# A fused stack of four layers on one core: the turns for the layer after the final norm move ahead of that norm, and one mixer's last splits and gates change place

## The chip, the cores and the metric

The kernel runs on 1 core of a Trainium2 chip. The time is the device time of one execution in microseconds (us), the median over runs. TensorE is PE in the profile (its weight loads are PEld), VectorE is DVE, ScalarE is ACT, GpSimd is POOL, and SyncE (SP) issues the weight transfers.

## The reference

`x` is 256 tokens by 1024 channels in float32. It goes through two stacks, one after the other. In short:

```python
def first_block(x, ...):
    for i in range(2):
        x = x + 0.5 * swiglu(rmsnorm(x, n1), wu1, wd1)
        h = rmsnorm(x, mix_norm[i])
        if i % 2 == 0:
            mix = mixer_delta_retention(h, ...)       # gated delta rule beside retention
        else:
            mix = mixer_dilated_differential(h, ...)
        x = x + mix
        x = x + 0.5 * swiglu(rmsnorm(x, n2), wu2, wd2)
    return rmsnorm(x, final_norm)

def second_block(x, ...):
    # layer 0
    hn = _rms_norm(h, e_norm_mix[i]);  ...  # gated unit beside an rwkv time mix
    h = h + _swiglu(_rms_norm(h, e_norm_ffn[i]), ...)
    # layer 1: sparse attention beside a short convolution, then 8 experts, 2 per token
    return _rms_norm(h, final_norm)
```

`rmsnorm(x, w)` is `x * rsqrt(mean(x*x) + 1e-6) * w`. The output of the first stack is normed by `final_norm`, and the first thing that the second stack does is to norm that again by `e_norm_mix`. The output of the delta mixer is, per head, normed, multiplied by a gate, and then multiplied by `l0_w_out`; the retention half has its own norm and gate.

## The kernel before, in words

`NETWORK` lists twelve layers: ffn 0, delta 1, ffn 2, ffn 3, attention 4, ffn 5, final 6, rwkv 7, ffn 8, sparse 9, moe 10, final 11 (the numbers are `at` in the code). Weights stream from HBM in steps of 128 x 3072 floats through a ring of three slots (`ring`, transfers issued at L3535 and L3541). Each step has three parts of 1024 columns. A float32 product is made from three passes of fp32r operands (L315 to L317: high by high, and the two high by low), so each part of each step is *split*: ACT rounds it to `w_hi` (`split_hi`, L283), then DVE subtracts for `w_lo` (`split_lo`, L290, parts 0 and 1) and POOL does the third part (`split_lo_last`, L296). PE waits for part 0 ahead of the first of a step's eight k blocks, for part 1 ahead of k = 2 and for part 2 ahead of k = 5.

The activations are wanted channel by partition, so PE transposes `X` by the identity (`head_tensor`, L406, 16 transposes in four pairs), ACT rounds and scales by the norm's gain (`head_scalar`, L414, 8 instructions) and DVE makes the low half (`head_vector`, L423, 8). The row norm itself is left out of the operand: PE multiplies the unscaled activations, while ACT sums the squares of `X` (`stats_scalar`, L432, L435), DVE takes the reciprocal (`stats_vector`, L442) and makes two diagonal matrices (L445), and PE turns these into a row (`row_tensor`, L452). In a mixer that begins with "t" tiles, as delta and rwkv do, `row_tensor` stands in PE's order between step 0 and step 1 of the projection. In DVE's order the split of step 1 stands ahead of `stats_vector`; in ACT's order the third part of step 1 (`split_hi(..., (2,))`) waits for the reciprocal.

Layer "final" (6) has nothing on PE. ACT sums squares per half of the tokens (`norm_scalar`, L337 to L344), DVE takes the reciprocal and overwrites `X` with the normed and gained rows (L348, L908). Only then does PE transpose `X` for rwkv; ahead of that it issues 16 matmuls whose result nobody uses (`keep_warm`, L329).

Delta's end: `inverse_tensor` and its partners on DVE and ACT invert eight 128 x 128 triangles in six levels. Each level is a product Y (L999), a copy by ACT (L960), a product dU (L1011), a subtraction by DVE (L937), a transpose back (L990) and a copy by DVE (L945). `ahead={...}` puts other DVE work ahead of a level's subtraction and `at_level={...}` puts other work into the level's middle. In level 6 PE turns retention's gated outputs of both token tiles (`turns((0, 1), 4)`, L1086) between Y and dU. After the levels come the delta rule's own products, a gate per token tile (`normalise`) and the output projection, whose first step `g` and second step `g + 1` are split meanwhile. `out_part` and `rest` are its products; the last of them, `rest(1)`, waits for the turned and split tile "delta hT 1 0".

## Time and profile before

| | |
|---|---|
| median of 3 runs | 2033.1 us (2032.88 to 2034.56) |
| the profiled execution | 2032.94 us, its span 2031.0 us |
| PE busy | 98% of the span |
| DVE, ACT, POOL busy | 76%, 57%, 20% |
| mean busy share of the DMA engines | about 57% |
| PE's granted clock over the span | 0.993 of full |

A timeline row gives the start, the length, the engine, the line, the operation, what is written and read, the count of instructions that are merged in the row, and in brackets how long the engine stood idle before it and for whom. PE's clock has two levels, 1.2 and 2.4 GHz; a granted clock of 0.5 is the lower.

### The profile page before, as it was taken

The page shows a single profiled execution, that of the slowest core. Times are in us where ns is not written, and L with a number is a line of the kernel's source. Part 1 is how long each engine was busy: PE and PEld are TensorE (multiplying, and loading weights), DVE is VectorE, ACT ScalarE, POOL GpSimd, SP SyncE. Part 2 cuts the span into 40 slices and gives each one's busy share as a digit, 9 for nine tenths or more (in the row PEclk, how much of TensorE's full clock was granted, in tenths as well). Part 3 has the DMA queues.
Part 4 walks back from the last instruction along what each step waited for, and adds up shares of the span by engine and source line. Part 5 has one row for each costly group of instructions (what it writes and reads, how often), then busy time and mean ns, then how long its engine had stood idle before and what let it go on. Part 6 is the DMA issues. An engine that isn't in the chain of part 4 may idle for free.

```text
span 2031.0 us, 31723 instructions
## 1 busy us (share of the span) xinstructions
PE 1981.4 (98%) x11697; PEld 1747.0 (86%) x11697; DVE 1551.4 (76%) x2173; ACT 1152.6 (57%) x1707; POOL 396.9 (20%) x192
## 2 busy tenths in 40 slices
PE   8999998999999999999999999999999999999997
PEld 6888998888888899988889898888998788888885
DVE  6777886777777778677778767777786798888886
ACT  5445664544554455654456535444566677777775
POOL 2222032322222310233222341322002000000000
PEclk9999999999999999999999999999999999999998
DMA  9555531555565544455544004555553688888895
GB/s 354 188 190 191 171 110 63 187 193 193 173 192 195 192 167 156 146 187 186 187 168 164 1 1 167 197 191 192 186 207 116 238 315 324 320 328 325 327 333 183
DMA packets 73395, 401.21 MB, mean 198 GB/s; under 512 B 8256, under 2 KB 8384, under 8 KB 41152
## 3 DMA queue, kind: packets, MB, share of 16 engines
q1 hardware_dynamic: 72848, 398.07, 56.3%
q8 instruction: 76, 1.25, 0.2%
q10 hardware_dynamic: 432, 1.57, 0.2%
q14 instruction: 39, 0.32, 0.0%
HBM read 398.57 MB, written 1.05 MB: 197 GB/s over the span
## 4 chain that ended last, share of the span: by engine, by line
PE 86%; DVE 8%; PEld 3%; ACT 2%; issue 1%; DMA 0%; SPq 0%; ACTq 0%; DVEq 0%; PEldq 0%
PE psum L777 20%; PE psum L315 15%; PE psum L316 14%; PE psum L317 14%; PE psum L757 10%; PE psum L1011 2%; DVE w_lo L290 2%; PE psum L999 2%; PE psum L3102 1%; PEld psum L315 1%; PEld psum L317 1%; PEld psum L316 1%; PE psum L329 1%; DVE w_lo L296 1%; PE psum L2358 1%
## 5 line engine op out<-in xcount | busy, mean ns | idle before, releaser
L290 DVE TENSOR_TENSOR w_lo<-ring,w_hi 128x1024 fp32r<-128x1024 f32 x498 | 739.7, 1515 | 175.2 <-ACT w_hi L283 173.9
L283 ACT ACTIVATE w_hi<-ring 128x1024 fp32r<-128x1024 f32 x744 | 739.9, 1051 | 206.1 <-PEq L509 106.2
L296 POOL TENSOR_TENSOR w_lo<-ring,w_hi 128x1024 fp32r<-128x1024 f32 x132 | 326.0, 2470 | 1098.0 <-ACT w_hi L283 1098.0
L777 PE MATMUL psum<-fT,w_hi 128*128 128x512 f32 x1760 | 421.9, 391 | 3.8 <-ACT w_hi L283 3.8
L777 PEld LDWEIGHTS psum<-fT,w_hi 128*128 128x128 f32 x1760 | 330.3, 189 | 72.0 <-ACT w_hi L283 4.2
L315 PE MATMUL psum<-w_hi,hT_hi 128*128 128x384 f32 (+4 forms) x896 | 321.1, 358 | 4.4 <-DVE hT_lo L1325 2.0
L317 PE MATMUL psum<-w_hi,hT_lo 128*128 128x384 f32 (+4 forms) x896 | 310.3, 346 | 0.0
L316 PE MATMUL psum<-w_lo,hT_hi 128*128 128x384 f32 (+4 forms) x896 | 310.0, 346 | 0.0
L315 PE MATMUL psum<-w_hi,act_hi 128*128 128x512 f32 x596 | 234.5, 393 | 0.8 <-DVE act_lo L3382 0.7
L757 PEld LDWEIGHTS psum<-fT,w_lo 128*128 128x128 f32 x1760 | 226.0, 191 | 8.9
L316 PE MATMUL psum<-w_lo,act_hi 128*128 128x512 f32 x596 | 233.5, 392 | 0.0
L317 PE MATMUL psum<-w_hi,act_lo 128*128 128x512 f32 x596 | 232.4, 390 | 0.0
L757 PE MATMUL psum<-fT,w_lo 128*128 128x256 f32 x1760 | 228.7, 283 | 0.0
L842 ACT ACTIVATE up_sums<-psum 128x512 f32<-128x512 f32 x110 | 65.6, 596 | 234.4 <-PE psum L757 234.4
L315 PEld LDWEIGHTS psum<-w_hi,hT_hi 128*128 128x128 f32 x896 | 169.3, 189 | 22.0 <-DVE w_lo L290 5.7
L317 PEld LDWEIGHTS psum<-w_hi,hT_lo 128*128 128x128 f32 x896 | 169.1, 189 | 13.5
L316 PEld LDWEIGHTS psum<-w_lo,hT_hi 128*128 128x128 f32 x896 | 169.6, 189 | 9.8 <-issue 0.2
L296 DVE TENSOR_TENSOR w_lo<-ring,w_hi 128x1024 fp32r<-128x1024 f32 x113 | 137.7, 1218 | 2.0 <-ACT w_hi L283 2.0
L844 ACT ACTIVATE silu<-silu 128x256 f32<-128x256 f32 x110 | 45.9, 417 | 162.8 <-DVE silu L876 162.8
L317 PEld LDWEIGHTS psum<-w_hi,act_lo 128*128 128x128 f32 x596 | 112.0, 188 | 24.5
L315 PEld LDWEIGHTS psum<-w_hi,act_hi 128*128 128x128 f32 x596 | 112.4, 189 | 23.4 <-issue 2.0
L316 PEld LDWEIGHTS psum<-w_lo,act_hi 128*128 128x128 f32 x596 | 112.4, 189 | 19.1
(507 smaller groups left out, 2384.2 us busy)
## 6 DMA issues: line engine op xcount, KB each, us to landing
ring<-in_stream SPq DMA_DIRECT2D x249, 1024.0 KB, 5.4
ring<-in_stream SPq DMA_DIRECT2D x248, 512.0 KB, 4.3
tables<-in_tables SPq DMA_DIRECT2D x1, 2261.0 KB, 19.8
gain_row<-in_gains ACTq DMA_DIRECT2D x3, 512.0 KB, 3.7
rows<-in_rows SPq DMA_DIRECT2D x1, 1288.0 KB, 22.7
X<-in_x SPq DMA_DIRECT2D x1, 1024.0 KB, 4.9
result<-X SPq DMA_DIRECT2D x2, 512.0 KB, 3.3
columns<-in_columns SPq DMA_DIRECT2D x1, 993.0 KB, 15.0
```

The source lines that it names most:

```text
L283: act.activation(part(w_hi, g, i), ring[:, k, i * PART:(i + 1) * PART], ACT.Copy) \
L290: dve.tensor_tensor(part(w_lo, g, i), ring[:, k, i * PART:(i + 1) * PART], part(w_hi, g, i).bitcast(F32), ALU.subtract) \
L296: pool.tensor_tensor(part(w_lo, g, 2), ring[:, k, 2 * PART:STEP], part(w_hi, g, 2).bitcast(F32), ALU.subtract) \
L315: pe.matmul(out_, w[0], x[0], start=first, stop=False, skip_group_check=True)
L316: pe.matmul(out_, w[0], x[1], start=False, stop=False, skip_group_check=True)
L317: return pe.matmul(out_, w[1], x[0], start=False, stop=last, skip_group_check=True)
L757: ins = pe.matmul(psum[:, 4 + 2 * (s % 2) + o, 0:SEQ], w[1][:, o, k, :], fT_hi[:, k, :], start=False, stop=k == KT - 1, skip_group_check=True)
L777: pe.matmul(psum[:, 4 + 2 * (s % 2) + o, :], w[0][:, o, k, :], fT[:, k, :, :].rearrange("p a c -> p (a c)"), start=k == 0, stop=False, ski ...
L842: act.activation(up_sums[:, s % 2, :, :], up_half(s, 1), ACT.Copy).then_inc(ffn_extra_kept, 1)
L844: act.activation(silu[:, s % 2, :], silu[:, s % 2, :], ACT.Silu).then_inc(ffn_silu_ready, 1)
L999: ins = pe.matmul(b[:, m * P:(m + 1) * P], AM[:, 4 * c + m, :], U[:, 4 * c + m, :], start=True, stop=True)
L1011: ins = pe.matmul(b[:, m * P:(m + 1) * P], T[:, 4 * c + m, :], Y[:, 4 * c + m, :], start=True, stop=True)
```

## The change

It has two parts. **Around the final norm**: PE's 16 transposes for rwkv (layer 7) read `X` as ffn 5 leaves it, ahead of the final norm, right after ffn 5's last product. The rounding then scales by `joint_gain`, the product of the two gains, computed once on DVE. The final norm of `X` is done behind these on ACT and DVE, as rwkv's row factor needs the squares of the normed `X`; that factor is then multiplied by the final norm's own (`rstd_f`), one DVE instruction more. The 16 `keep_warm` matmuls go. **In delta's end**: retention's gate of the second token tile (`retention_gated(1)`, 4 instructions) stands ahead of level 6 instead of level 5; part 0 of step `g` is split behind the levels instead of ahead of level 6; its third part is split by POOL, once level 5 is done, instead of by DVE; and for step `g + 1` the turned tile's rounding and its low half stand ahead of the last part that each of ACT and DVE splits.

```diff
@@ rstd_vector @@
-            dve.reciprocal(rstd[:, t:t + 1], rms[:, t:t + 1]).then_inc(*norm.vector())
+            dve.reciprocal(rstd_f[:, t:t + 1], rms[:, t:t + 1]).then_inc(*norm.vector())
@@ gain_of @@
+        def after_final(n):
+            return n > 0 and NETWORK[n - 1][0] == "final"
+
         def gain_of(n):
+            if after_final(n):
+                return joint_gain
             return columns[:, KT * NETWORK[n][1]:KT * (NETWORK[n][1] + 1)]
@@ head_tensor @@
-                        pe.wait_ge(*after(f"x {n} {t} {k}"))
+                        pe.wait_ge(*after(f"x {n - after_final(n)} {t} {k}"))
@@ stats_vector @@
             dve.reciprocal(rstd[:, :], rms[:, :]).then_inc(*norm.vector(f"norm {n} rstd"))
             dve.wait_ge(*norm.vector.so_far())
+            if after_final(n):
+                dve.tensor_tensor(rstd[:, :], rstd[:, :], rstd_f[:, :], ALU.mult).then_inc(*norm.vector(f"norm {n} rstd"))
+                dve.wait_ge(*norm.vector.so_far())
@@ ffn_tensor @@
-            if NETWORK[at + 1][0] != "final":
-                head_tensor(pe, at + 1)
+            head_tensor(pe, at + 1 + (NETWORK[at + 1][0] == "final"))
@@ final_vector @@
             for t in range(TT):
                 rstd_vector(dve, at, t)
-            for t, ins in enumerate(gained(dve, at, X)):
+            dve.wait_ge(*after(f"norm {at + 1} turn {PAIRS[-1]}"))
+            for t, ins in enumerate(gained(dve, at, X, rstd_f)):
@@ delta_scalar @@
-            split_hi(act, g + 1, g + 1)
+            split_hi(act, g + 1, g + 1, (0, 1))
             turned_hi(1, 0)
+            split_hi(act, g + 1, g + 1, (2,))
@@ delta_pool @@
             inverse_pool(pool, "delta", d_A, d_AM)
-            out_pool(pool, at, first=1)
+            pool.wait_ge(*after(f"delta U {LEVELS - 2} 1"))
+            out_pool(pool, at)
@@ delta_vector @@
-            def retention_gated():
-                dve.wait_ge(*after("delta ret root"))
-                does(None, dve.reciprocal, d_ret_rms, d_ret_rms)
-                dve.wait_ge(*after("delta rg"))
-                settle()
-                for t in range(TT):
+            def retention_gated(t):
+                if t == 0:
+                    dve.wait_ge(*after("delta ret root"))
+                    does("delta ret inverse", dve.reciprocal, d_ret_rms, d_ret_rms)
+                    dve.wait_ge(*after("delta rg"))
+                    settle()
+                for t in (t,):
...
-                           ahead={2: retention_scores, 3: weighted_gate, 4: retention_sums, 5: retention_gated, 6: lambda: split_lo(dve, g, g, (0,))})
+                           ahead={2: retention_scores, 3: weighted_gate, 4: retention_sums, 5: lambda: retention_gated(0), 6: lambda: retention_gated(1)})
             turned_lo(0, 4)
             turned_lo(1, 4)
-            split_lo(dve, g, g, (1,))
-            dve.wait_ge(hi_last_ready, g + 1)
-            dve.tensor_tensor(part(w_lo, g, 2), ring[:, in_ring(g, g)[0], 2 * PART:STEP], part(w_hi, g, 2).bitcast(F32), ALU.subtract) \
-               .then_inc(lo_last_ready, 1)
+            split_lo(dve, g, g)
...
-            split_lo(dve, g + 1, g + 1)
+            split_lo(dve, g + 1, g + 1, (0,))
             turned_lo(1, 0)
+            split_lo(dve, g + 1, g + 1, (1,))
@@ tensor block @@
-                elif NETWORK[at - 1][0] == "final":
-                    keep_warm(pe, psum[:, 7, :], 16)
-                    head_tensor(pe, at)
@@ scalar block @@
                         load_gain_row(act, n)
+                        head_scalar(act, at + 1)
                         norm_scalar(act, at)
@@ vector block @@
+                    dve.tensor_tensor(joint_gain[:, :], col("gain")[:, KT * 6:KT * 7], col("gain")[:, KT * 10:KT * 11], ALU.mult) \
+                       .then_inc(*norm.vector("joint gain"))
                 if kind == "final":
                     if NETWORK[at - 1][0] != "moe":
+                        head_vector(dve, at + 1)
                         final_vector(dve, at)
```

On DVE, from the end of ffn 5 to rwkv's first copies, before:

```order
L894 SCALAR_TENSOR_TENSOR X<-psum,rstd_f,X 128x512 x4
L348 RECIPROCAL rstd<-rms 128x1 x2
L908 SCALAR_TENSOR_TENSOR X<-X,rstd,gain_row 128x1024 x2
L423 SCALAR_TENSOR_TENSOR hT_lo<-psum,columns,hT_hi 128x256 x8
L2634 MEMSET r_pb 128x14
L2634 TENSOR_TENSOR columns<-columns,tables 128x512
L290 TENSOR_TENSOR w_lo<-ring,w_hi 128x1024 x2
L442 RECIPROCAL rstd<-rms 128x2
L445 TENSOR_SCALAR O<-tables,rstd 128x128 x2
```

and in the changed kernel, whose lines stand some numbers further down:

```order
L905 SCALAR_TENSOR_TENSOR X<-psum,rstd_f,X 128x512 x4
L432 SCALAR_TENSOR_TENSOR hT_lo<-psum,joint_gain,hT_hi 128x256 x8
L349 RECIPROCAL rstd_f<-rms 128x1 x2
L919 SCALAR_TENSOR_TENSOR X<-X,rstd_f,gain_row 128x1024 x2
L2647 MEMSET r_pb 128x14
L2647 TENSOR_TENSOR columns<-columns,tables 128x512
L291 TENSOR_TENSOR w_lo<-ring,w_hi 128x1024 x2
L451 RECIPROCAL rstd<-rms 128x2
L454 TENSOR_TENSOR rstd<-rstd,rstd_f 128x2
L457 TENSOR_SCALAR O<-tables,rstd 128x128 x2
```

The eight low halves of the turned `X` moved ahead of the final norm's three steps; the split of rwkv's step 1 still stands between the final norm and the diagonals.

On ACT at the same place, before:

```order
L283 ACTIVATE w_hi<-ring 128x1024 x3
L901 DMA gain_row<-in_gains 128x1024
L337 ACT_TABLE_LOAD
L337 ACTIVATE warm<-tables 128x1
L341 ACTIVATE O,squares<-X 128x1024
L344 ACTIVATE rms<-squares,tables 128x1
L341 ACTIVATE O,squares<-X 128x1024
L344 ACTIVATE rms<-squares,tables 128x1
L414 ACTIVATE hT_hi<-psum,columns 128x256 x8
L429 ACTIVATE warm<-tables 128x1
L432 ACTIVATE O,squares<-X 128x1024 x2
```

and in the changed kernel:

```order
L284 ACTIVATE w_hi<-ring 128x1024 x3
L912 DMA gain_row<-in_gains 128x1024
L423 ACTIVATE hT_hi<-psum,joint_gain 128x256 x8
L338 ACT_TABLE_LOAD
L338 ACTIVATE warm<-tables 128x1
L342 ACTIVATE O,squares<-X 128x1024
L345 ACTIVATE rms<-squares,tables 128x1
L342 ACTIVATE O,squares<-X 128x1024
L345 ACTIVATE rms<-squares,tables 128x1
L438 ACTIVATE warm<-tables 128x1
L441 ACTIVATE O,squares<-X 128x1024 x2
```

The eight roundings moved ahead of the table load and the final norm's squares.

On DVE in delta's last levels (levels 5 and 6 and what follows), before:

```order
L1325 RECIPROCAL d_small<-d_small 128x8
L1325 SCALAR_TENSOR_TENSOR O<-O,d_small,d_tok 128x128 x8
L937 TENSOR_TENSOR d_U<-d_U,psum 128x512 x2
L945 COPY d_T<-psum 128x512 x2
L290 TENSOR_TENSOR w_lo<-ring,w_hi 128x1024
L937 TENSOR_TENSOR d_U<-d_U,psum 128x512 x2
L1325 TENSOR_TENSOR hT_lo<-psum,hT_hi 128x4x128 x2
L290 TENSOR_TENSOR w_lo<-ring,w_hi 128x1024
L1473 TENSOR_TENSOR w_lo<-ring,w_hi 128x1024
L1325 COPY O<-psum 128x512
```

and in the changed kernel:

```order
L1339 RECIPROCAL d_small<-d_small 128x8
L1339 SCALAR_TENSOR_TENSOR O<-O,d_small,d_tok 128x128 x4
L949 TENSOR_TENSOR d_U<-d_U,psum 128x512 x2
L957 COPY d_T<-psum 128x512 x2
L1339 SCALAR_TENSOR_TENSOR O<-O,d_small,d_tok 128x128 x4
L949 TENSOR_TENSOR d_U<-d_U,psum 128x512 x2
L1339 TENSOR_TENSOR hT_lo<-psum,hT_hi 128x4x128 x2
L291 TENSOR_TENSOR w_lo<-ring,w_hi 128x1024 x2
L1339 COPY O<-psum 128x512
```

Four of the eight gate instructions took the place of the split ahead of the last subtraction; behind it two splits stand as before, and the third is gone to POOL.

## Rows read from the trace of the kernel before

**Rows 1.** The page: busy time of PE, and the chain that ended last, by engine.

```profile
PE 1981.4 (98%) x11697; PEld 1747.0 (86%) x11697; DVE 1551.4 (76%) x2173; ACT 1152.6 (57%) x1707; POOL 396.9 (20%) x192
PE 86%; DVE 8%; PEld 3%; ACT 2%; issue 1%; DMA 0%; SPq 0%; ACTq 0%; DVEq 0%; PEldq 0%
```

**Rows 2.** Timeline from ffn 5's last product to rwkv's first.

```profile
1038.24 0.61 PE L802 MATMUL psum<-w_hi,act_lo 128*128 128x512 f32 x2
...
1039.01 3.61 PE L329 MATMUL psum<-tables 128*128 128x512 bf16 x16
...
1041.27 1.04 ACT L341 ACTIVATE O<-X 128x1024 f32<-128x1024 f32 x1
...
1043.03 2.48 DVE L908 SCALAR_TENSOR_TENSOR X<-X,rstd,gain_row 128x1024 f32<-128x1024 f32 x2
...
1048.63 0.37 PE L315 MATMUL psum<-hT_hi,w_hi 128*128 128x256 f32 x1
```

**Rows 3.** Timeline of rwkv's first two steps, engine by engine.

```profile
1047.38 3.37 DVE L423 SCALAR_TENSOR_TENSOR hT_lo<-psum,columns,hT_hi 128x256 fp32r<-128x256 f32 x8 [1.86 <-ACT hT_hi L414]
...
1051.27 2.36 DVE L290 TENSOR_TENSOR w_lo<-ring,w_hi 128x1024 fp32r<-128x1024 f32 x2
...
1053.74 0.48 DVE L445 TENSOR_SCALAR O<-tables,rstd 128x128 f32<-128x128 f32 x2
...
1054.88 2.39 POOL L296 TENSOR_TENSOR w_lo<-ring,w_hi 128x1024 fp32r<-128x1024 f32 x1 [15.82 <-ACT w_hi L283]
...
1056.89 0.61 PE L452 MATMUL psum<-O,tables 128*128 128x128 f32 x4
...
1059.10 0.28 PE L315 MATMUL psum<-hT_hi,w_hi 128*128 128x256 f32 x1
```

**Rows 4.** Timeline of another passage, from ffn 0 straight to delta.

```profile
198.81 0.62 PE L802 MATMUL psum<-w_hi,act_lo 128*128 128x512 f32 x2
...
201.54 0.36 PE L315 MATMUL psum<-hT_hi,w_hi 128*128 128x256 f32 x1
...
199.97 3.03 ACT L414 ACTIVATE hT_hi<-psum,columns 128x256 fp32r<-128x256 f32 x8 [0.95 <-PE psum L406]
203.01 1.28 ACT L429 ACT_TABLE_LOAD   x1
```

**Rows 5.** Timeline of delta's levels 5 and 6, and of its end.

```profile
322.40 2.19 DVE L1325 SCALAR_TENSOR_TENSOR O<-O,d_small,d_tok 128x128 f32<-128x128 f32 x8
...
328.23 0.69 DVE L945 COPY d_T<-psum 128x512 f32<-128x512 f32 x1 [0.64 <-PE psum L990]
...
347.32 0.68 DVE L1325 TENSOR_TENSOR hT_lo<-psum,hT_hi 128x512 fp32r<-128x512 f32 x1
...
343.65 2.94 ACT L283 ACTIVATE w_hi<-ring 128x1024 fp32r<-128x1024 f32 x3
...
325.29 1.13 PE L999 MATMUL psum<-d_U,d_pad 128*128 128x128 f32 x8 [1.89 <-issue]
...
328.02 1.04 PE L1086 MATMUL psum<-tables,O 128*128 128x128 f32 x8
328.90 1.95 PE L1011 MATMUL psum<-d_Y,d_T 128*128 128x128 f32 x16
...
345.46 0.60 PE L1086 MATMUL psum<-tables,O 128*128 128x128 f32 x4
348.06 0.45 PE L315 MATMUL psum<-w_hi,hT_hi 128*128 128x384 f32 x1 [2.00 <-DVE hT_lo L1325]
```

**Rows 6.** Windows: span of time, its length, busy time by engine, PE's granted clock.

```profile
349.00:352.00 3.00, 3.00 (x11) 3.00 (x10) 0.33 (x1) 0.00 (x0) 0.64 (x1) 0.50 0.84 344
...
1045.10:1048.40 3.30, 2.83 (x14) 2.84 (x15) 1.44 (x4) 1.87 (x5) 0.00 (x0) 0.51 0.00 0
```

**Rows 7.** Timeline of one step of ffn 5, POOL and DVE side by side.

```profile
1028.37 2.41 POOL L296 TENSOR_TENSOR w_lo<-ring,w_hi 128x1024 fp32r<-128x1024 f32 x1 [5.87 <-ACT w_hi L283]
...
1029.27 3.72 DVE L290 TENSOR_TENSOR w_lo<-ring,w_hi 128x1024 fp32r<-128x1024 f32 x2 [1.37 <-ACT w_hi L283]
```

More of the change, by code:

```diff
@@ L68, in __getitem__ @@
         return slice(*self.at[name])
-COLUMN = Places([("gain", 10 * KT), ("conv", 4 * 12), ("mu", 14), ("w0", 4), ("a0", 4), ("k_k", 4), ("k_a", 4),
+COLUMN = Places([("gain", 11 * KT), ("conv", 4 * 12), ("mu", 14), ("w0", 4), ("a0", 4), ("k_k", 4), ("k_a", 4),
                  ("r_k", 4), ("sgu_b", 4), ("sgu_w", 4 * P), ("router", KT * EXPERTS), ("lora", 512), ("g2", 512),
@@ L137, in network_kernel @@
         rstd_f = sb("rstd_f", [P, TT])
+        joint_gain = sb("joint_gain", [P, KT])
         rstd_diag = O[:, 0, 0:TT * P].rearrange("p (t c) -> p t c", t=TT)
@@ L411, in head_scalar @@
                 act.wait_ge(*after(f"norm {n} turn {p}"))
+                if after_final(n):
+                    act.wait_ge(*after("joint gain"))
                 for i in range(2):
@@ L443, in stats_vector @@
             dve.wait_ge(*norm.vector.so_far())
+            if after_final(n):
+                dve.tensor_tensor(rstd[:, :], rstd[:, :], rstd_f[:, :], ALU.mult).then_inc(*norm.vector(f"norm {n} rstd"))
+                dve.wait_ge(*norm.vector.so_far())
             for t in range(TT):
@@ L901, in load_gain_row, with gained @@
             act.dma_start(gain_row[:, :], gains_in[which].partition_broadcast(P)).then_inc(row_loaded, 16)
-        def gained(dve, at, to):
+        def gained(dve, at, to, scale=rstd):
             dve.wait_ge(row_loaded, 16 * sum(kind in ("final", "moe") for kind, _ in NETWORK[:at + 1]))
             for t in range(TT):
-                yield dve.scalar_tensor_tensor(to[:, t, :], X[:, t, :], rstd[:, t:t + 1], gain_row[:, :], ALU.mult, ALU.mult)
+                yield dve.scalar_tensor_tensor(to[:, t, :], X[:, t, :], scale[:, t:t + 1], gain_row[:, :], ALU.mult, ALU.mult)
         def final_vector(dve, at):
@@ L3473, in _ @@
                         load_gain_row(act, n)
+                        head_scalar(act, at + 1)
                         norm_scalar(act, at)
                 elif kind != "moe":
-                    head_scalar(act, at, (3,) if after_mixer(at) else PAIRS)
+                    if not after_final(at):
+                        head_scalar(act, at, (3,) if after_mixer(at) else PAIRS)
                     if at == 0:
@@ L3498, in _ @@
                 if kind != "moe":
-                    head_vector(dve, at, (3,) if after_mixer(at) else PAIRS)
+                    if not after_final(at):
+                        head_vector(dve, at, (3,) if after_mixer(at) else PAIRS)
                     if at == 0:
@@ L3666, in pack_columns @@
     names = ["l0_ffn1_norm", "l0_mix_norm", "l0_ffn2_norm", "l1_ffn1_norm", "l1_mix_norm", "l1_ffn2_norm",
-             "e_norm_mix_2", "e_norm_ffn_2", "o_norm_mix_2", "o_norm_ffn_2"]
+             "e_norm_mix_2", "e_norm_ffn_2", "o_norm_mix_2", "o_norm_ffn_2", "final_norm"]
     c[:, COLUMN["gain"]] = np.concatenate([per(a[n].reshape(-1)) for n in names], axis=1)
```

## The prediction

> **What bounds the kernel now.** I read the page first, then the timeline where the change lies, then the windows for the clock. The page says that PE is busy for 98% of the span and that 86% of the chain that ended last is PE's [rows 1]. So a change can only give back time in which PE waits or runs at its lower clock; work taken from DVE or ACT counts for nothing by itself. There are two such places where the diff lies.
>
> The first is around the final norm. PE issues ffn 5's last product at 1038.24 and rwkv's first at 1048.63. Between them it runs 16 matmuls for nobody (3.61 us), then waits for ACT's squares and DVE's 2.48 us of rewriting `X`, since the transposes read the rewritten `X` [rows 2]. In the same trace ffn 0 passes straight to delta with the same 16 transposes: last product 198.81, first product 201.54, 2.73 us instead of 10.39 [rows 4].
>
> The second is delta's end. Y of level 6 starts at 325.29 after 1.89 us of idle, behind DVE's eight gate instructions (2.19 us), and the last product of the first output step starts at 348.06 after 2.00 us of idle [rows 5]. Behind that second gap the granted clock is 0.50, the level of 1.2 GHz; so it is behind the gaps of the final norm [rows 6].
>
> **The change, at the final norm.** The passage becomes that of ffn 0, moved by 1038.24 - 198.81 = 839.43. rwkv's first product then starts at 201.54 + 839.43 = 1040.97, 7.66 us earlier than now. The 16 idle matmuls cost nothing more. That is not the gain yet, because the row factor stands next in PE's order, 8.26 us after the first product (1048.63 to 1056.89 [rows 2, 3]): PE asks for it at about 1049.3, and it is now late. Its chain:
>
> - ACT ends the eight roundings and loads its table at 203.01 + 839.43 = 1042.44 for 1.28 us [rows 4]. That load was hidden under ffn 5's end before. The first square starts at about 1043.8. The second follows a square of 1.04 us, its reading and its root; I take 1.35, so 1045.15. From the second square's start to the rewriting of `X` took 1043.03 - 1041.27 = 1.76 [rows 2], so DVE starts at 1046.9 and ends 2.48 later, at 1049.4.
> - DVE then has the same work as now between the low halves and the diagonals: 1047.38 + 3.37 = 1050.75 to 1053.74, 2.99 us, of which 2.36 are the split of step 1 [rows 3]. ACT's second pair of squares ends beneath that split. The added multiplication of two columns I take at 0.25 us with its wait (bounds 0.1 and 0.5, the lengths of nothing but a small instruction and of both diagonals, 0.48). The diagonals start at 1052.65 and are done at 1053.1, against 1054.22 now.
> - So PE stands idle at the row from about 1049.3 to 1053.2, some 3.9 us, where before it did not wait.
> - Behind the row, step 1 wants its third part at k = 5, which it reaches 1059.10 - 1056.89 = 2.21 us after the row [rows 3]: 1055.4. But ACT rounds that part only after the reciprocal and the multiplication, and POOL's 2.39 us follow; POOL starts 1.14 after the diagonals start (1053.74 to 1054.88), so at 1053.8, and ends at 1056.2 [rows 3]. With a handover of 0.1, k = 5 starts at 1056.3, against 1059.10.
>
> That is 2.8 us, not 7.66. What the clock takes has to come off: behind gaps of two to three microseconds the lower clock lasted 3.3 us [rows 6], and this gap is longer. If it begins at the row, 3.3 us pass before full speed is back, half of it lost; PE has 0.9 us of slack to the third part, so 0.7 remains. I take 0.65, with bounds 0 (all of it falls in the gaps) and 1.65 (none does). The part gives 2.8 - 0.65 = 2.15. Queues passed: SP's transfers wait for the splits, which come earlier; the gain row's transfer stands before the moved roundings as before. The joint gain's instruction lies on DVE while it waits for ACT's first rounding behind ffn 0, and costs at most 0.1.
>
> **The change, in delta's end.** Four gate instructions are 1.10 us, so Y of level 6 starts at 324.2. But the other four stand now between DVE's last copy (328.92, now 327.8) and PE's turn of the second tile, which stands ahead of dU. The gate ends at 328.9, four transposes take half of 328.90 - 328.02, 0.44, and dU starts at 329.4: 0.5 us later than now, and not earlier [rows 5]. DVE then has two splits ahead of the copy of `o 0` as it had before, so everything behind comes 0.5 later. POOL's split of the third part begins at about 324.8 and is done by 327.8, long before PE asks; nothing waits for it.
>
> At the end ACT rounds the turned tile after two parts instead of three (0.98 us each). PE's transposes end at 345.46 + 0.60 = 346.06; from ACT being free to the low half took 347.32 - (343.65 + 2.94) = 0.73, and from there to PE's product 348.06 - 347.32 = 0.74 [rows 5]. So 347.5 instead of 348.06, plus the 0.5 from above: 348.0. The path gains 0.05 and the gap shrinks from 2.0 to 1.45 us. The two parts split later, ACT's third and POOL's behind it, are done at about 351.5 with the 0.5; PE asks for them near 352.6 at full clock.
>
> What remains is the clock. In three microseconds at 0.50 PE does half the work [rows 6]; 3.3 us minus the stretch's edges cost 1.5. The gap of 1.89 us ahead of level 6 was followed by full-length work at the higher clock (eight matmuls in 1.13, as elsewhere), the one of 2.00 was not [rows 5]. With 1.45 I expect the clock to stay up, and take 1.5 us; bounds 0 and 1.6.
>
> **Sum.** 2.15 + 0.05 + 1.5 = 3.7, less 0.1 for the joint gain: 3.6. Against the profiled execution's 2032.94 that is 2029.3; the median of the runs, 2033.1, is 0.16 above it, so I forecast 2029.4, 0.18% faster. A measurement of this kernel can tell about 0.2%, 4.1 us, from no change, so the likeliest case lies just inside "the same".
>
> A rule that speaks against the change: the Trainium skill, TensorE: Matmul & The Clock Gate, "Why this matters for your kernels", wants no long idle gap between bursts of matmuls, since the array falls back to its lower clock. The trace agrees: both low stretches follow gaps, one of them only 2.0 us long. By that rule the removed 16 matmuls and the new gap at the row are a risk, priced in the third rival.
>
> A second one: the Trainium skill, SBUF — State Buffer, "Who interferes with whom", says that POOL and a DVE instruction with both inputs in SBUF exclude each other for a whole instruction. The trace agrees: beside POOL's split, DVE's pair takes 3.72 us, and 2.36 with POOL idle [rows 3, 7]. What that pair of rows prices here, 1.4 us, would hit the gate ahead of level 6 only if POOL's split began 0.6 us or more later than I work out.
>
> **Rivals.**
> - *The row does not hold PE* (5%): had the diagonals come by 1049.3, all 7.66 would stand and the time be 2023.7. Against it: DVE's order above leaves no way around the two rewrites and the split. A partial form, no clock lost at the row (10%), gives 2028.7.
> - *Delta gives nothing* (20%): its last gap still drops the clock, or POOL's split lands on the gate (the 1.4 us above): 2029.4 + 1.5 = 2030.9.
> - *The gaps that the change opens bring the clock down each time* (5%, the other side): at the row for two low stretches instead of one, 6.6 us at half speed, 3.3 lost less 0.9 of slack and more behind it, some 3.3 in all against the 0.65; in delta a new gap of 1.4 us ahead of dU costs another 1.6, and the end keeps its own 1.5. 2029.4 + 2.65 + 1.6 + 1.5 = 2035.2. It decides from 3.7 us of extra loss on. For it: the longer idle time at the row. Against it: no gap under 2.0 us had this effect.
> - *The norm's chain is longer than worked out* (12%): each microsecond on ACT or DVE between the table load and the diagonals is one of PE. With 2 more, 2031.4.
>
> **The numbers.** The worked-out case has 48%, with 2028.3 to 2030.5 as its own range. For eight in ten I take 2027.4 to 2031.7, which leaves out the full gain and the other side. Faster by over 0.2% means under 2029.0: 0.36 (a part of the likeliest case, the first rival and its partial form). Within 0.2%: 0.60. Slower: 0.04.
>
> **What would show it.** In the trace of the changed kernel: rwkv's first product 2.7 us behind ffn 5's last; PE idle for about 4 us ahead of the row's matmuls; the DVE split of step 1 right behind the rewritten `X`; POOL's split ending just as PE resumes at k = 5; in delta, Y of level 6 after a gap under 1 us, a new gap ahead of the second tile's transposes of 1.4 us, and the last gap at 1.4 us with the clock at full behind it. The prediction fails if the row arrives early, or if the clock's low stretches lie otherwise than assumed: they are a third of the sum.

## The result, and the profile after

The changed kernel took 2037.44 us (median of 14 runs, 2035.91 to 2041.47) against 2033.04 of the kernel before on the same chips (14 runs). The ratio is 1.0025, 95% interval 1.0018 to 1.0032: slower by 4.4 us, where the prediction had 2029.4 and a range up to 2031.7. The profiled execution took 2038.2 us. The first lines of its page (span; busy time of PE; the shares of the chain that ended last):

```profile
span 2036.1 us, 31697 instructions
...
PE 1985.4 (98%) x11681; PEld 1751.9 (86%) x11681; DVE 1550.5 (76%) x2174; ACT 1153.0 (57%) x1707; POOL 399.8 (20%) x193
...
PE 85%; DVE 8%; PEld 3%; ACT 2%; issue 1%; DMA 0%; POOL 0%; SPq 0%; PEldq 0%; DVEq 0%; ACTq 0%
```

PE's share of span and chain is what it was [rows 1], and the span is 5.1 us longer. So the first question is whether the two places that the change is about went otherwise than worked out. Line numbers are shifted in the new kernel, by one at L283 to L317 and by 7 to 14 further down. Timeline at the final norm (start, length, engine, line, operation, count, and idle time with its releaser):

```profile
1037.18 0.47 PE L810 MATMUL psum<-w_hi,act_hi 128*128 128x512 f32 x1 [0.45 <-DVE act_hi L893]
...
1042.20 0.37 PE L316 MATMUL psum<-hT_hi,w_hi 128*128 128x256 f32 x1
...
1051.26 2.35 DVE L291 TENSOR_TENSOR w_lo<-ring,w_hi 128x1024 fp32r<-128x1024 f32 x2
...
1053.72 0.16 DVE L454 TENSOR_TENSOR rstd<-rstd,rstd_f 128x2 f32<-128x2 f32 x1
...
1053.92 0.48 DVE L457 TENSOR_SCALAR O<-tables,rstd 128x128 f32<-128x128 f32 x2
...
1054.45 0.71 PE L464 MATMUL psum<-O,tables 128*128 128x128 f32 x4 [3.31 <-DVE O L457]
...
1055.05 2.39 POOL L297 TENSOR_TENSOR w_lo<-ring,w_hi 128x1024 fp32r<-128x1024 f32 x1 [14.68 <-ACT w_hi L284]
...
1057.49 0.39 PE L316 MATMUL psum<-hT_hi,w_hi 128*128 128x256 f32 x1 [0.55 <-POOL w_lo L297]
```

The sum's steps stand here almost word for word. rwkv's first product comes at 1042.20, 2.63 us behind the start of the last product of ffn 5 (1039.57) in place of 10.4 (1048.63 less 1038.24 [rows 2]). The diagonals come from DVE at 1053.92, behind the two splits and the one multiplication more; PE waits 3.31 us for them, and at k = 5 POOL's third of the split binds by 0.55. Against ffn 5's first last-step product (1037.18; 1035.88 before, so 1.30 late) the product at k = 5 is early, 1057.49 for 1059.10 [rows 3]: the part gave 2.9 us.

Timeline of delta's end, PE alone:

```profile
325.80 1.13 PE L1011 MATMUL psum<-d_U,d_pad 128*128 128x128 f32 x8 [0.83 <-issue]
...
330.62 0.63 PE L1098 MATMUL psum<-tables,O 128*128 128x128 f32 x4 [1.49 <-DVE O L1339]
...
339.10 1.13 PE L1186 MATMUL psum<-d_rhs,d_U 128*128 128x128 f32 x8 [0.42 <-DVE d_rhs L1339]
...
349.74 0.44 PE L316 MATMUL psum<-w_hi,hT_hi 128*128 128x384 f32 x1 [1.41 <-DVE hT_lo L1339]
```

In front of level 6 the new kernel is 1.57 us late (312.79 for 311.22 in the level before). At 325.80 it is only 0.51 late, so Y of level 6 is 1.06 earlier by itself; the second tile's turn then waits 1.49 for the gate, and the last product, behind a gap of 1.41, is 1.68 late. The path gave nothing and cost 0.1.

Windows of time, with PE's granted clock in the third column from the right:

```profile
350.00:351.00 1.00, 1.00 (x7) 1.00 (x7) 1.00 (x2) 0.00 (x0) 1.00 (x1) 1.00 0.00 0
351.00:352.00 1.00, 1.00 (x8) 1.00 (x7) 0.28 (x1) 0.00 (x0) 1.00 (x1) 1.00 0.17 25
...
1045.00:1048.00 3.00, 3.00 (x27) 3.00 (x27) 0.16 (x1) 2.92 (x8) 0.00 (x0) 1.00 0.00 0
...
1104.00:1107.00 3.00, 3.00 (x24) 2.67 (x21) 2.83 (x4) 0.00 (x0) 0.00 (x0) 0.52 0.72 289
...
1131.00:1134.00 3.00, 2.21 (x10) 2.24 (x11) 1.17 (x2) 1.30 (x4) 0.08 (x1) 0.57 0.03 5
...
1578.00:1584.00 6.00, 5.55 (x47) 5.02 (x47) 3.80 (x5) 5.38 (x14) 4.30 (x5) 1.00 0.00 0
```

The low stretches of before [rows 6] are gone in both places. In their stead two others appear, at 1104 and 1131, while one of before's, at 1577.6 to 1584.5, is not there. And between the places the new kernel loses time steadily, with no wait to show for it: 1.0 us over delta's projections (190 to 300), 0.9 over attention's (740 to 845), 2.1 over sparse's (1454 to 1570), 2.3 over the MoE (1649 to 1990). In the FFN's stretches it loses nothing. The form of the loss is seen in groups of the projections' matmuls, here of the changed kernel (count, busy us and mean ns of one):

```profile
L317 PE MATMUL psum<-w_lo,hT_hi 128*128 128x512 f32 x320 | 126.0, 394 | 0.0
...
L317 PE MATMUL psum<-hT_lo,w_hi 128*128 128x256 f32 x336 | 94.7, 282 | 0.0
```

and in the same two groups of a kernel that has the same instructions at other addresses (e6 below):

```profile
L318 PE MATMUL psum<-w_lo,hT_hi 128*128 128x512 f32 x320 | 125.4, 392 | 0.0
...
L318 PE MATMUL psum<-hT_lo,w_hi 128*128 128x256 f32 x336 | 93.8, 279 | 0.0
```

Each matmul takes 2 to 3 ns more. The mean column is a matmul's whole duration, of which most lies beside its neighbours; what counts is the distance between the starts of two successive ones, the pitch. I took it from the timeline, as a mean over all pairs of equal shape that stand back to back at full clock: with hT moving (256 columns, w stationary) 115.4 ns in before and 119.0 after; with w moving in 384 columns 174.7 and 177.0, in 512 columns 229.8 and 232.7. Over the 1008, 1200 and 960 such matmuls of the three passes that is 3.6 + 2.8 + 2.8 us, and 10.0 with the smaller groups. That is more than the four stretches above show (6.3); where the rest went was not measured.

What differs for these matmuls is nothing in the order. The change grows `columns` by 32 bytes a partition and adds `joint_gain`, 32 more (two lines of the change that the diff above leaves out; e1 shows them). Everything allotted behind them moves: w_hi from byte 125120 to 125184, w_lo, act and fT with it by 64, while hT_hi (61568) and hT_lo stay. The experiments call w_hi less hT_hi modulo 256 the *distance*: 64 before, 128 after. (The expectation of e1 names the operands of the 256-column group the wrong way round: there hT moves and w is stationary.)

### The profile page after: what moved, and what is told of

Its sections match the earlier page's. It is cut to its first block, busy times and chain, and to the rows that moved or that the text cites. A ratio compares the mean times of both kernels' runs of the same rounds, so it can differ in the third digit from the quotient of the medians.

```text
span 2036.1 us, 31697 instructions
## 1 busy us (share of the span) xinstructions
PE 1985.4 (98%) x11681; PEld 1751.9 (86%) x11681; DVE 1550.5 (76%) x2174; ACT 1153.0 (57%) x1707; POOL 399.8 (20%) x193
## 3 DMA queue, kind: packets, MB, share of 16 engines
q10 hardware_dynamic: 432, 1.57, 0.2%
## 4 chain that ended last, share of the span: by engine, by line
PE 85%; DVE 8%; PEld 3%; ACT 2%; issue 1%; DMA 0%; POOL 0%; SPq 0%; PEldq 0%; DVEq 0%; ACTq 0%
PE psum L789 20%; PE psum L316 14%; PE psum L318 14%; PE psum L317 14%; PE psum L769 10%; DVE w_lo L291 2%; PE psum L1011 2%; PE psum L1023 2%; PE psum L3115 1%; PEld psum L316 1%; PEld psum L318 1%; PEld psum L317 1%; DVE w_lo L297 1%; PE psum L2371 1%; PE psum L1002 1%
## 5 line engine op out<-in xcount | busy, mean ns | idle before, releaser
L317 PE MATMUL psum<-w_lo,hT_hi 128*128 128x384 f32 (+4 forms) x896 | 310.9, 347 | 0.0
L317 PE MATMUL psum<-w_lo,act_hi 128*128 128x512 f32 x596 | 233.5, 392 | 0.0
L317 PEld LDWEIGHTS psum<-w_lo,hT_hi 128*128 128x128 f32 x896 | 169.4, 189 | 10.6 <-issue 0.2
L317 PEld LDWEIGHTS psum<-w_lo,act_hi 128*128 128x128 f32 x596 | 112.4, 189 | 19.4
```

Source lines behind the costliest of these rows:

```text
L317: pe.matmul(out_, w[0], x[1], start=False, stop=False, skip_group_check=True)
```

## The experiments

**e1: before's instructions at the new addresses.**

```diff
-COLUMN = Places([("gain", 10 * KT), ...
+COLUMN = Places([("gain", 11 * KT), ...
+        joint_gain = sb("joint_gain", [P, KT])
-             "e_norm_mix_2", "e_norm_ffn_2", "o_norm_mix_2", "o_norm_ffn_2"]
+             "e_norm_mix_2", "e_norm_ffn_2", "o_norm_mix_2", "o_norm_ffn_2", "final_norm"]
```

> The kernel before with every instruction as it was, and only the changed kernel's two additions to the SBUF (columns 10*KT to 11*KT floats, a joint_gain tile that nothing uses), so that w_hi, w_lo and the whole arena lie 64 bytes higher, at the addresses of the changed kernel. Placement theory: the pitch of the projections' matmuls with 256 moving columns (hT the weights) goes from 115.4 to about 119.0 ns, that of 384 columns from 174.7 to 177, that of 512 from 229.8 to 232.7, and the time is 7 to 10 us above the kernel before, about 2041. Rivals (the order of the instructions or their place in the instruction stream is what costs, or the chip's day): the pitches stay at 115.4, 174.7 and 229.8 and the time is within 1 us of the kernel before.

2039.28 us against 2033.01; ratio 1.0029 (1.0018 to 1.0039), pitches 118.9, 176.9 and 232.8, and in its page the two groups above stand word for word as in the changed kernel (126.0 and 94.7 us). The added bytes, which no instruction needs, cost 6.3 us (3.7 to 7.9 by the interval). The order of the instructions is not the cause.

**e2: the changed kernel, 64 bytes further.**

```diff
+        spare = sb("spare", [P, 16])
```

> The changed kernel with an unused tile of 64 bytes a partition behind joint_gain, so that w_hi and w_lo lie 128 bytes above their place in the kernel before, at the same offset in a line of 128 bytes. Placement theory: the three pitches are back at 115.4, 174.7 and 229.8 ns, and the time is that of the changed kernel less 7 to 10 us: about 2029, 4 us below the kernel before, which is what the prediction's sum gave. Rivals: nothing changes, 2037, pitches 119, 177 and 232.7.

2033.95 us, ratio 1.0004 (0.9995 to 1.0013): 3.5 us less than the changed kernel, not 7 to 10. Pitches 117.3, 176.0 and 232.9: other ones, but not those of before. So the theory as I had put it, a line of 128 bytes, fell; the addresses remained.

**e4 and e5: each part alone.** e4 is before with delta's hunks only, no address moved; e5 before with the final norm's hunks and the spare tile of e2.

> The kernel before with the part of the change in delta alone (gate of tile 1 at level 6, POOL's third of the split, turned copies ahead), no address moved. The prediction's sum: 1.5 us below the kernel before, by the clock, with 0.05 on the path. Comparison of the two traces: the path through delta got no shorter (shift +1.57 us ahead of level 6, +1.68 at the last product), and only the low stretch of the clock behind it went (1.4 us), so -1.4 if it goes here as well and within 0.3 us of before if it does not. If the order of the instructions were what makes the projections slower: some us above before.

> The kernel before with the part of the change at the final norm alone and the unused 64 bytes, so that w_hi and w_lo keep their offset in a line of 128 bytes. The prediction's sum: 2.1 us below before. Comparison of the two traces: rwkv's row matmuls at k=4 came about 2.9 us earlier against what stood ahead, and the clock did not fall: 2.5 to 3 us below before, about 2030.3. If the order of the instructions were what makes the projections slower: some us above before.

e4: 2029.75 us, ratio 0.9983 (0.9974 to 0.9992), 3.3 us faster. Its timeline:

```profile
323.90 1.13 PE L999 MATMUL psum<-d_U,d_pad 128*128 128x128 f32 x8 [0.83 <-issue]
...
328.71 0.63 PE L1086 MATMUL psum<-tables,O 128*128 128x128 f32 x4 [1.49 <-DVE O L1327]
...
347.75 0.45 PE L315 MATMUL psum<-w_hi,hT_hi 128*128 128x384 f32 x1 [1.41 <-DVE hT_lo L1327]
```

It enters level 5 at -0.34 us against before, stands at +0.28 behind the turn and at -0.31 at the last product (347.75 for 348.06): so the path lost 0.03, where the prediction had it gain 0.05; then it gains 1.55 us by 353 (shift -1.86), because the clock stays up. e5: 2036.94 us, ratio 1.0019 (1.0009 to 1.0028), slower. Its pitches are e2's (117.9, 175.9, 233.0). By the pitches these are worth 6 to 7 us, and the part itself would have given about 3; by e2 against e6 (below), the same instructions at these two distances, they are worth 4.9, which leaves 1.0. So e5 does not price the part; e10 does it directly.

**e6: the changed kernel with the arena back.** Each small tile takes 32 bytes; three of one element made one give 64 back.

```diff
-        warm, warm_exp, warm_silu = (sb(n, [P, 1]) for n in ("warm", "warm_exp", "warm_silu"))
+        warms = sb("warms", [P, 3])
+        warm, warm_exp, warm_silu = (warms[:, i:i + 1] for i in range(3))
```

> The changed kernel, with the three one-element warm tiles made one tile of three elements, which gives back the 64 bytes: w_hi, w_lo and the whole arena stand where they stand in the kernel before, and only rows and tables stay 32 bytes higher. Placement theory (the pitches belong to the place of the arena): 115.4, 174.7 and 229.8 ns again, and both parts of the change give what they gave apart: 3.3 us for delta (measured alone, nothing moved) and 2.9 us for the final norm (its part of the comparison of the traces), about 2027, 6 us below before. Rival (the pitches belong to the place of rows and tables or to the order of the instructions at the final norm): the pitches of the changed kernel, 2033 to 2037.

2028.62 us (2026.02 to 2030.26) against 2032.58; ratio 0.9980 (0.9972 to 0.9989): 4.0 us faster than before and 8.8 below the changed kernel (8.4 with each set against its own runs of before), by three one-element tiles made one. Pitches 115.2, 174.7, 229.8. Windows of this trace:

```profile
1050.00:1051.00 1.00, 0.00 (x0) 0.00 (x0) 0.96 (x3) 0.00 (x0) 0.00 (x0) 1.00 0.00 0
...
1052.00:1053.00 1.00, 1.00 (x6) 1.00 (x6) 0.15 (x1) 0.10 (x1) 0.82 (x1) 0.50 0.82 156
1053.00:1054.00 1.00, 1.00 (x7) 1.00 (x6) 0.97 (x4) 0.00 (x0) 1.00 (x1) 0.50 0.94 385
...
1055.00:1056.00 1.00, 1.00 (x11) 1.00 (x10) 0.09 (x1) 1.00 (x2) 0.00 (x0) 1.00 0.46 98
...
348.00:352.00 4.00, 4.00 (x23) 4.00 (x24) 2.04 (x3) 0.57 (x2) 3.09 (x1) 1.00 0.46 129
324.00:332.00 8.00, 6.44 (x55) 6.17 (x56) 4.34 (x10) 2.39 (x4) 2.35 (x1) 1.00 0.00 0
```

Here the clock falls in the gap at the row (0.50 at 1052 to 1054; the four row matmuls, row below, take 1.23 us in place of 0.71), and in delta it does not.

```profile
1051.59 1.23 PE L465 MATMUL psum<-O,tables 128*128 128x128 f32 x4 [3.57 <-DVE O L458]
```

**e7 to e9: which distance.** Before with 64 unused bytes ahead of the ring (e7), with them between X and hT_hi (e8), and with the warm tiles made one, so that the arena stands 64 lower (e9).

> The kernel before with an unused tile of 64 bytes ahead of the ring, so that every tile moves by 64 bytes and no distance between two of them changes. If the distance between hT and w (or the ring and w) is what sets the pitches: 115.4, 174.7 and 229.8 ns and the time of before. If the absolute place of w_hi and w_lo does: 119, 177 and 232.8 ns and 6 us above before.

> The kernel before with the unused 64 bytes between X and hT_hi: the ring and X stay, hT, O and the arena move by 64. If the distance between hT and w sets the pitches: 115.4, 174.7 and 229.8 ns, 2033. If that between the ring and w, or the absolute place of w, does: 119, 177 and 232.8 ns, 2039.

> The kernel before with the three warm tiles made one and nothing else: the arena alone stands 64 bytes lower. If a line of 128 bytes is what counts (w at 0 in it, as when it stands 64 higher): 119, 177 and 232.8 ns, 2039. If one of 256 bytes counts: something else than those, since the offset in it is 128, a fourth one beside 192 of before, 0 and 64.

e7: 2034.58, ratio 1.0007 (0.9998 to 1.0016). e8: 2033.16, 1.0001 (0.9992 to 1.0010). Both have before's pitches, with w_hi at byte 125184, where it stands in the changed kernel. e9: 2038.34, 1.0030 (1.0019 to 1.0041), and pitches 119.9, 174.9 and 229.7: the group with hT moving is slow, that with w moving is not.

```profile
L317 PE MATMUL psum<-w_lo,hT_hi 128*128 128x512 f32 x320 | 125.1, 391 | 0.0
...
L317 PE MATMUL psum<-hT_lo,w_hi 128*128 128x256 f32 x336 | 95.0, 283 | 0.0
```

So in the projections neither the absolute place nor the ring counts, and the two groups have different wishes.

**e10: the final norm alone, the arena back.**

> The part of the change at the final norm alone, with the three warm tiles made one, so that the arena stands where it stands in the kernel before (final norm alone with the arena 128 bytes higher took 2036.9). Distance theory: pitches of before, 115.4, 174.7 and 229.8 ns, and the part's own worth: the prediction's 2.15 us below before if the clock falls in the idle gap at the row matmuls, as it did in the kernel with both parts and the arena back, and up to 2.9 if it does not: 2030 to 2031. Rival (this part costs time of its own): 2033 or above.

2030.84 us against 2032.77, ratio 0.9994 (0.9985 to 1.0003): 1.9 us by the medians and 1.2 by the ratio, not to be told from none by this measurement alone, and not against the 2.15. Its trace leads before by 3.1 us more behind the row than ahead of it; there the clock stayed up.

**e11 to e13: the measure and its steps.** `rows` and `tables` allotted ahead of hT_hi, which moves hT by 115 times 256 bytes (e11); the arena 32 bytes higher (e12) and lower (e13).

> The kernel before with rows and tables allotted ahead of hT_hi: the arena stays, hT_hi and hT_lo move up by 29440 bytes, an odd number (115) of 256 bytes. If the distance from hT to w counts modulo 256 bytes: 115.4, 174.7 and 229.8 ns and the time of before. If it counts in a longer measure (512 bytes or more), or if the neighbourhood of other tiles counts: other pitches and up to 6 us more or less.

> The kernel before with an unused tile of 32 bytes ahead of the arena: the distance from hT_hi to w_hi modulo 256 is 96 (64 in before, 128 and 192 and 0 in the kernels so far). Between the pitches of 64 and 128 if they change gradually: 117 ns for 256 columns, 231 for 512, 2 to 4 us above before; those of 64, and the time of before, if blocks of 64 bytes count.

> The kernel before with the warm tiles made one and 32 bytes unused: the distance modulo 256 is 32. If blocks of 64 bytes count: those of distance 0, 119.9 ns for 256 columns and 229.7 for 512, 2038. If it changes gradually: about 117.5 ns and 2035.

e11: 2031.87, 1.0001 (0.9992 to 1.0010), before's pitches: the distance counts modulo 256 at most. e12: 2042.23, 1.0041 (1.0028 to 1.0055), 118.2, 177.6 and 233.2 ns. e13: 2036.63, 1.0020 (1.0011 to 1.0029), 118.4, 175.5 and 232.8. Neither of the forms I had offered, blocks of 64 or a gradual change, fits: at distance 96 the kernel is slowest though both neighbours are better.

**e15, e16: hT or what lies behind it.** The warm tiles made one, and 64 bytes ahead of hT_hi (e15) or between hT_lo and O (e16).

> The kernel before with 64 bytes ahead of hT_hi and the three warm tiles made one: hT and O stand 64 bytes higher, the arena stays. Distance modulo 256 is 0, as in the kernel with the arena 64 bytes lower: 119.9 ns for hT moving, 229.7 for w moving, about 2038, 5 us above before. If the place of w itself counts: before's pitches, 2033.

> The kernel before with 64 bytes between hT_lo and O and the warm tiles made one: O, columns, rows and tables stand 64 bytes higher, hT and the arena stay. Distance theory: 115.4, 174.7, 229.8 ns and the time of before. If O or columns against w count: about 5 us more.

e15: 2039.69, 1.0028 (1.0016 to 1.0040), pitches 119.9, 174.9, 229.6, e9's. e16: 2031.96, 0.9995 (0.9986 to 1.0004), 113.9, 174.5, 229.9. It is hT against w.

**e14: the pitch by itself.** Behind the last store, PE runs the three passes over slices of w_hi and w_lo that begin d floats further on; nothing of it enters the output.

```diff
+        def measure_hw(pe, d):
+            w = [x[:, 0, :] for x in (w_hi, w_lo)]
+            for j in range(2):
+                for k in range(KT - 1):
+                    three_passes(pe, psum[:, j, 0:COLS], [x[:, k, j * P:(j + 1) * P] for x in (hT_hi, hT_lo)],
+                                 [x[:, k * COLS + d:(k + 1) * COLS + d] for x in w], k == 0, k == KT - 2)
```

> The kernel before, and behind its last store four stretches of TensorE alone that only measure (their sums go nowhere; the output is the reference's): three passes over hT and w, first w moving (384 columns, hT stationary, 42 matmuls for each distance), then hT moving (256 columns, w stationary, 21 matmuls for each), at distances w less hT of 64, 96, 128, 160, 192 and 0 bytes modulo 256. The first stretch with nothing beside it, the second with VectorE's splits, the third with ScalarE's roundings, the fourth with both and DMAs into the ring. If the two reads of TensorE alone make the pitch: in the first stretch hT moving takes 115.4 ns at 64, about 118 at 96, 119 at 128, 117.5 at 192, 120 at 0, and w moving 174.7 at 64 and 0, 177 at 128. 
One run, 2298.28 us with the measuring. Windows, each one group of matmuls from its first start to that of the next (42 with w moving, distances 64, 96, 128 and 160; then 21 with hT moving, 64 and 128), first with nothing beside them, then from 2235 on with VectorE, ScalarE and DMAs at work:

```profile
2040.06:2047.39 7.33, 7.33 (x44) 7.33 (x43) 0.00 (x0) 0.00 (x0) 0.00 (x0) 1.00 0.00 0
2047.39:2054.81 7.42, 7.42 (x44) 7.42 (x43) 0.00 (x0) 0.00 (x0) 0.00 (x0) 1.00 0.00 0
2054.81:2062.20 7.39, 7.39 (x43) 7.39 (x43) 0.00 (x0) 0.00 (x0) 0.00 (x0) 1.00 0.01 2
2062.20:2069.49 7.29, 7.29 (x44) 7.29 (x43) 0.00 (x0) 0.00 (x0) 0.00 (x0) 1.00 0.00 0
...
2084.11:2086.58 2.47, 2.47 (x22) 2.47 (x22) 0.00 (x0) 0.00 (x0) 0.00 (x0) 1.00 0.00 0
...
2089.05:2091.57 2.52, 2.52 (x24) 2.52 (x23) 0.00 (x0) 0.00 (x0) 0.00 (x0) 1.00 0.00 0
...
2235.23:2242.56 7.33, 7.33 (x44) 7.33 (x43) 6.96 (x6) 6.94 (x7) 0.00 (x0) 1.00 0.56 163
2242.56:2249.98 7.42, 7.42 (x44) 7.42 (x43) 7.21 (x7) 7.20 (x8) 0.00 (x0) 1.00 0.74 264
...
2257.38:2264.66 7.28, 7.28 (x43) 7.28 (x43) 7.07 (x7) 7.09 (x7) 0.00 (x0) 1.00 0.65 241
...
2279.28:2281.76 2.48, 2.48 (x23) 2.48 (x23) 2.41 (x3) 2.42 (x3) 0.00 (x0) 1.00 0.29 76
...
2284.22:2286.74 2.52, 2.52 (x24) 2.52 (x22) 2.45 (x3) 2.46 (x3) 0.00 (x0) 1.00 0.51 127
```

With nothing beside PE: w moving 7.33 / 42 = 174.5 ns at 64 (173.4 without one start-to-start distance of 228 ns at the head of that group), 176.7 at 96, 176.0 at 128, 173.6 at 160; hT moving 2.47 / 21 = 117.6 at 64 and 120.0 at 128. The last five windows have DVE and ACT busy nearly all the time and 160 to 260 GB/s of DMA in the long ones, and the same lengths to 0.01 us. So the effect is there with TensorE alone, and these other engines do not change it. With w moving it repeats the kernels' order: 64 and 0 alike (173.4), 128 and 96 slower. With hT moving it does so in part only: 128 is slower than 64, by 2.2 ns in place of 3.6, but 64, 96 and 192 come out alike within 0.5 ns, where the kernels have 115.4, 118.2 and 117.3. So this is a check that TensorE alone shows a dependence on the place of w, and no table for planning.

**e17: the same for the FFN.** fT, the FFN's moving operand, is at distance 0 in all kernels above. e6 with 192 bytes ahead of it makes that 64.

> The changed kernel with the arena back (2028.6 in an earlier run), and 192 unused bytes ahead of fT, so that w_hi and w_lo less fT is 64 modulo 256 (0 in every kernel so far). If the FFN's matmuls with fT moving follow the same rule: those with 256 columns (1760 recorded, pitch 119 now) go towards 115.4, those with 512 columns stay, up to 6 us less: 2022 to 2026. If something else binds them: 2028.6.

2029.28 us, ratio 0.9980 (0.9971 to 0.9990), e6's time. Groups of e6 (line, operation, count, busy, mean ns), then of e17:

```profile
L790 PE MATMUL psum<-fT,w_hi 128*128 128x512 f32 x1760 | 421.6, 391 | 3.8 <-ACT w_hi L285 3.8
...
L318 PE MATMUL psum<-w_lo,act_hi 128*128 128x512 f32 x596 | 233.3, 392 | 0.0
...
L770 PE MATMUL psum<-fT,w_lo 128*128 128x256 f32 x1760 | 228.7, 283 | 0.0
```

```profile
L791 PE MATMUL psum<-fT,w_hi 128*128 128x512 f32 x1760 | 433.5, 396 | 4.1 <-ACT w_hi L286 4.1
...
L771 PE MATMUL psum<-fT,w_lo 128*128 128x256 f32 x1760 | 219.1, 277 | 0.0
```

The form with 256 columns got 9.6 us shorter and that with 512 columns 11.9 longer, where the expectation had it stay. Places count in the FFN too, with opposite wishes of the two forms, and not with the projections' numbers: there 512 columns take the same time at 0 and at 64.

**e18, e19: places chosen by the rule.** w_lo 64 bytes further from w_hi, all behind it by 256 (e18), and that with the arena 64 lower (e19).

```diff
-            w_hi, w_lo = (take(n, [P, 2, STEP], F32R) for n in ("w_hi", "w_lo"))
+            w_hi = take("w_hi", [P, 2, STEP], F32R)
+            take("w_between", [P, 16])
+            w_lo = take("w_lo", [P, 2, STEP], F32R)
+            take("w_behind", [P, 48])
```

> The changed kernel with the arena back (2028.6), and w_lo moved up by 64 bytes against w_hi, all behind it by 256: w_hi less fT is 0 and w_lo less fT 64 modulo 256, w_hi less hT stays 64 and w_lo less hT becomes 128. If the rule holds matmul by matmul: the FFN's form with 256 columns takes 9.6 us less (228.7 to 219.1 busy), that with 512 columns stays at 421.6, and the projections lose about 3.2 us in their third with w_lo (3.6 ns by 336, 2.3 by 400 and 3 by 320 of each pass): 2022, 6 us below the kernel it is built on and 10 to 11 below before. If the gain of one form is taken back by the other whatever their distances: 2028 to 2032.

> As the kernel before it in this call, with the arena 64 bytes lower: w_hi less hT is 0 and w_lo less hT 64, the FFN's distances unchanged. By the pitches measured at 0 (119.9 against 115.4 ns for hT moving, 174.9 and 229.7 for w moving) the projections lose 4.5 ns in two thirds of 1008 matmuls, 3.0 us, and nothing where w moves: 2022, within 1 us of the kernel with 64 and 128.

Both expectations were wrong by 15 us and more: 2037.52 (1.0020, 1.0010 to 1.0029) and 2039.58 (1.0031, 1.0020 to 1.0042). e18:

```profile
L793 PE MATMUL psum<-fT,w_hi 128*128 128x512 f32 x1760 | 421.6, 391 | 3.8 <-ACT w_hi L288 3.8
...
L321 PE MATMUL psum<-w_lo,act_hi 128*128 128x512 f32 x596 | 235.2, 395 | 0.0
L322 PE MATMUL psum<-w_hi,act_lo 128*128 128x512 f32 x596 | 234.6, 394 | 0.0
L773 PE MATMUL psum<-fT,w_lo 128*128 128x256 f32 x1760 | 225.8, 281 | 0.0
```

and e19:

```profile
L771 PE MATMUL psum<-fT,w_lo 128*128 128x256 f32 x1760 | 225.8, 281 | 0.0
```

The form with 256 columns got 2.9 us shorter in both, not 9.6. And the groups with act stationary, whose pitch was 229.2 in e6, stand at 232.5, all three passes of them (234.6 us for w_hi,act_lo in place of 232.2), though only one of the three has changed its own distance: 1788 of them make 5.9 us. So the distance between a matmul's own two operands is not the whole rule. A neighbour's operand, the weights loaded while a matmul streams, would be a candidate, but it is not the whole either. The FFN's matmuls with 256 columns stand sixteen in a row that read w_lo and fT and nothing else. In e17 and in e19 these two tiles stand at the same bytes (149696 and 186752), and still the pitch inside the rows is 114.1 ns in e17 and 117.7 in e19. What differs is where other tiles stand, w_hi (125120 and 125056) and act among them. Which of them counts, and how, no run here shows.

## Why the prediction was wrong

**The step that failed** is "less 0.1 for the joint gain". It priced the new tile by its instruction and the new column not at all, and never asked where they put what is allotted behind them. e1 gives the price of exactly that, 6.3 us; the changed kernel against e6 gives 8.4 to 8.8, and the pitches add up to 10.0. The three agree on the cause and not on the exact price. All other terms together came out right: e6, which is the change without the displacement, is 4.0 us faster than before (2.2 to 5.7 by its interval), 3.6 was forecast. That it is so near is in part luck: apart, the two parts measured 3.3 (e4, 1.6 to 5.3) and 1.9 (e10, at most 3.0), for 1.55 and 2.15. None of the rivals held this cause, so the range and the chances missed too: the other side, slower, had 4% for a clock that falls each time.

**The final norm, 2.8 less 0.65.** The 2.8 was right (2.9 in the changed kernel's trace, with first product, row, the two extra DVE operations and POOL as the next bound each in place; PE's wait came out at 3.31 to 3.57 us in place of 3.9). The clock's fall at the row is no matter of yes or no: of the eight traces with the new order it fell there in four (e2, e6, e17, e19) and stayed up in four (the changed kernel, e5, e10, e18). By the lead over before ahead of the row and behind it, the part gave 2.5 in e6, where the clock fell, and 3.1 in e10, where it did not. Half of the 0.65 would have been the better mean; no median here can tell.

The Trainium skill ("TensorE: Matmul & The Clock Gate", "Why this matters for your kernels") asks to keep idle gaps out of a matmul stream. The new order opens a gap of 3.3 us at the row where there was none, so by that rule alone the clock should have fallen behind it. It did in four of the eight traces; in the changed kernel's it stayed up, and the part gained 2.9 us there, since the gap took the place of the keep-warm matmuls and of the norm's chain ahead of the transposes.

**Delta, 0.05 on the path.** Right to within 0.2 us: in place of a gain of 0.05, a loss of 0.03 in e4 and of 0.11 in the changed kernel. Y of level 6 came 1.06 earlier (1.10 forecast), the turn then waited for the gate, and the last gap is 1.41 us (1.45 forecast).

**Delta, 1.5 by the clock.** Right in size in e4's trace (1.55), but the reading behind it was one that a single trace could not carry: I had read that the gap of 1.89 us ahead of level 6 leaves the clock up, and in the rivals that no gap under 2.0 us brings it down. Of 13 traces with the old order of delta's end, the clock fell at 348 to 356 in nine and at 324 to 332 in six, in at least one of the two in all but e1; of seven with the new order (gaps of 0.83, 1.49 and 1.41) in none. So the rival that delta gives nothing (20%) is excluded (e4 lies 1.6 to 5.3 us below before), and the change kept the clock up at level 6 as well as at the end, where the old order had six falls and nine. That each was the work of the gap beside it is argued from the counts; no run moved one of them alone.

**The clock elsewhere.** Stretches at 1104, 1131 and 1577 to 1588 come and go between traces of kernels that do not differ there, at 1 to 3 us each. The profiled execution of before had the one at 1577; the comparison of two single traces would have booked it to the change.

## What to carry to other kernels

A change that adds or grows an on-chip tile moves every tile allotted behind it, and that can cost more than the change gives: list the addresses of the operands before and after, and if they moved, measure the old instructions at the new addresses first. Put new small tiles behind the big ones or into the padding of others. When the starts of all matmuls of some groups lie 1 to 3% further apart and no wait shows, suspect where the operands stand as well as the order. Whether a chosen place is better has to be measured: e18 and e19 chose theirs by a rule and lost 9 to 11 us against e6.

Judge a term of the clock over several traces, since the same gap brings the clock down in some executions and not in others (at the row in four of eight).

## What the runs showed of the hardware

As long as w_hi and w_lo move together, the pitch of back-to-back matmuls in this kernel's projections goes with the distance between stationary and moving operand in the partition, modulo 256 bytes. Measured in whole kernels (ns with hT moving, 256 columns; w moving, 384; w moving, 512; and the time):

| distance | kernels | hT moving | w, 384 | w, 512 | us |
|---|---|---|---|---|---|
| 0 | e9, e15 | 119.9 | 174.9 | 229.7, 229.6 | 2038.3, 2039.7 |
| 32 | e13 | 118.4 | 175.5 | 232.8 | 2036.6 |
| 64 | before, e7, e8, e11, e16 | 113.9 to 115.5 | 174.4 to 174.7 | 229.8 to 229.9 | 2031.9 to 2034.6 |
| 96 | e12 | 118.2 | 177.6 | 233.2 | 2042.2 |
| 128 | changed kernel, e1 | 119.0, 118.9 | 177.0, 176.9 | 232.7, 232.8 | 2037.4 (with the change), 2039.3 |
| 192 | e2, e5 | 117.3, 117.9 | 176.0, 175.9 | 232.9, 233.0 | 2034.0 (with the change), 2036.9 (with its part at the norm) |

The Trainium skill ("SBUF — State Buffer", "Who interferes with whom") gives TensorE two read ports for the moving operand and the weights, calls them independent, and has one source of contention only, the port pair that VectorE and GpSimd share. In e14 TensorE alone, with no other engine at work, took 117.6 or 120.0 ns for the same matmuls according to where the weights began. The measurement decides: TensorE's pace is not independent of where its operands stand. Why is open, and so is why e18's groups with act became slower in all three passes, and what makes e17 and e19 differ over the same two tiles.
